# Modulation in units of 2048 columns, zero-padded half chunks, stick-breaking spread out, and two tiles computed together by chunk

## What is computed

```python
# first block, layer l (ctx is a second stream of 256 tokens, updated in layer 0 only)
mod = silu(c) @ w_mod[l] + b_mod[l]            # 1024 -> 6*1024, the same for ctx from c_ctx
sh1, sc1, g1, sh2, sc2, g2 = split(mod, 6)
h = rms_norm(x, norm1[l]) * (1 + sc1) + sh1
na_q, na_k, na_v, gq, gk, gv, ga, gb = split(h @ w_in[l])   # widths 512,512,512,512,128,128,1024,1024
ya = neighbourhood_and_ctx_attention(na_q, na_k, na_v)      # 8 heads
yb = softmax_attention(rope(norm(gq)), rope(norm(gk)), gv)  # 8 query, 2 key/value heads, x and ctx keys
x = x + g1 * ((sigmoid(ga) * (ya @ w_pa) + sigmoid(gb) * (yb @ w_pb)) @ w_o)
h2 = rms_norm(x, norm2[l]) * (1 + sc2) + sh2
x = x + g2 * ((silu(h2 @ w_a) * (h2 @ w_u)) @ w_out)        # hidden width 2816
# second block, layer l: half FFN, mixer, half FFN
x = x + 0.5 * ffn1(rmsnorm(x))
y_a = forgetting_attention(...)      # 6 heads
y_b = stick_breaking(...)            # 5 heads: log-sigmoids of the scores, summed over later keys
y_c = dsa(...)                       # 5 heads, keys of the top 64 by an index score
x = x + (g_a * (y_a @ w_up_fox) + g_b * (y_b @ w_up_sb) + g_c * (y_c @ w_up_dsa)) @ w_out
x = x + 0.5 * ffn2(rmsnorm(x))
```

## Time and profile before

| | |
|---|---|
| median of three runs | 2757.98 us |
| the profiled execution | 2758.39 us |
| its span in the trace | 2756.4 us |
| mean granted TensorE clock | 0.958 |
| TensorE busy | 2602.2 us (94%) |
| VectorE busy | 1367.5 us (50%) |
| ScalarE busy | 1144.9 us (42%) |
| GpSimd busy | 303.6 us (11%) |
| chain that ended last | TensorE 83%, ScalarE 7%, VectorE 6%, DMA 1% |

### The profile page before, as it was taken

One profiled execution on the slowest core, in us unless ns is written; L12 is line 12 of the kernel. 1 busy time (PEld: TensorE's weight loads), 2 busy tenths in 40 slices (PEclk: granted clock), 3 DMA queues, 4 the chain that ended last, 5 costly groups with the idle time before them and its releaser, 6 DMA issues.

```text
span 2756.4 us, 41454 instructions
## 1 busy us (share of the span) xinstructions
PE 2602.2 (94%) x17370; PEld 2281.8 (83%) x17370; DVE 1367.5 (50%) x2351; ACT 1144.9 (42%) x1970; POOL 303.6 (11%) x292
## 2 busy tenths in 40 slices
PE   4997999899999899989999998999999999999998
PEld 2763677677777687779999997889999998887998
DVE  2234434333333424555566556646556656665654
ACT  3242444322122424554454444445445444444543
POOL 1132411200000002410010000111000000022000
PEclk6997999899999889989999999989999999999999
DMA  5412222244443222235465452325545554333544
GB/s 223 177 54 94 75 77 92 92 183 164 180 183 132 90 85 90 80 123 183 167 207 184 168 193 99 131 100 170 184 168 198 179 173 155 115 118 137 182 166 140
DMA packets 60184, 393.44 MB, mean 143 GB/s; under 512 B 6688, under 2 KB 6848, under 8 KB 23520
## 3 DMA queue, kind: packets, MB, share of 16 engines
q1 hardware_dynamic: 59328, 384.45, 39.8%
q0 software_dynamic: 672, 6.36, 0.6%
HBM read 389.73 MB, written 1.05 MB: 142 GB/s over the span
## 4 chain that ended last, share of the span: by engine, by line
PE 83%; ACT 7%; DVE 6%; issue 2%; POOL 2%; DMA 1%; SPq 0%; DVEq 0%; POOLq 0%; ACTq 0%
PE ps L822 69%; PE ps L900 4%; DVE ring_lo L1459 3%; PE ps L972 2%; PE ps L863 2%; PE ps L957 2%; PE ps L946 1%; ACT w_hi L1109 1%; ACT logits L1249 1%; ACT prob_t L1164 1%; PE ps L873 1%; DMA ring<-w_mod 1%; PE ps L922 1%; DMA ring<-w_w_in 1%; PE ps L913 0%
## 5 line engine op out<-in xcount | busy, mean ns | idle before, releaser
L1459 DVE TENSOR_TENSOR ring_lo<-ring,w_hi 128x1024 fp32r<-128x1024 f32 (+3 forms) x712 | 764.6, 1115 | 553.1 <-ACT w_hi L1109 552.9
L822 PE MATMUL ps<-h_hi,w_hi 128*128 128x256 f32 (+1 forms) x3408 | 963.3, 314 | 30.5 <-ACT h_hi L1154 26.3
L822 PE MATMUL ps<-h_lo,w_hi 128*128 128x256 f32 (+1 forms) x3408 | 934.8, 307 | 0.0
L1109 ACT ACTIVATE w_hi<-ring 128x1024 fp32r<-128x1024 f32 (+3 forms) x712 | 642.7, 950 | 580.4 <-PE ps L822 232.8
L822 PEld LDWEIGHTS ps<-h_hi,w_hi 128*128 128x128 f32 x3408 | 654.5, 193 | 90.1 <-issue 31.0
L822 PEld LDWEIGHTS ps<-h_lo,w_hi 128*128 128x128 f32 x3408 | 652.7, 193 | 27.9
L822 PE MATMUL ps<-h_hi,ring_lo 128*128 128x256 f32 (+1 forms) x3408 | 558.3, 307 | 0.0
L822 PEld LDWEIGHTS ps<-h_hi,ring_lo 128*128 128x128 f32 x3408 | 484.8, 192 | 28.6
L822 PE MATMUL ps<-hid_hi,w_hi 128*128 128x256 f32 (+1 forms) x1056 | 284.2, 302 | 0.0
L822 PE MATMUL ps<-hid_lo,w_hi 128*128 128x256 f32 (+1 forms) x1056 | 283.4, 301 | 0.0
L1393 POOL TENSOR_SCALAR logits<-logits,stat 128x512 f32<-128x512 f32 (+2 forms) x140 | 161.3, 1165 | 738.2 <-DVE stat L1689 738.2
(11 more groups left out here) (222 smaller groups left out, 2435.8 us busy)
## 6 DMA issues: line engine op xcount, KB each, us to landing
ring<-w_ffn_in SPq DMA_DIRECT2D x132, 1024.0 KB, 4.8
ring<-w_ffn_out SPq DMA_DIRECT2D x96, 704.0 KB, 4.0
ring<-w_mod SPq DMA_DIRECT2D x48, 1024.0 KB, 6.8
ring<-w_in SPq DMA_DIRECT2D x42, 1024.0 KB, 4.8
ring<-w_w_in SPq DMA_DIRECT2D x30, 1024.0 KB, 4.9
ring<-w_up SPq DMA_DIRECT2D x16, 576.0 KB, 3.6
ring<-w_pab SPq DMA_DIRECT2D x8, 1024.0 KB, 4.8
ring<-w_wo SPq DMA_DIRECT2D x8, 1024.0 KB, 4.7
```

The source lines that it names most:

```text
L822: mm = pe.matmul(ps[f.bank][:, 0:n], (hi_w if wpart == "hi" else lo_w)[0:rows, at:at + P], hi if part == "hi" else lo, start=left == first ...
L1109: act.activation(w_hi[q.s % 2][:, h * n:(h + 1) * n], ring[q.slot][:, h * n:(h + 1) * n], ACT.Copy)\
L1459: dve.tensor_tensor(ring_lo[q.slot][:, c], ring[q.slot][:, c], plain(w_hi[q.s % 2][:, c]), ALU.subtract)\
```

## The change

- **Modulation.** A unit is 2048 columns of eight chunks; each chunk is one piece of four matmuls (one per group of 512 columns, each group in its own 32 array columns), all in bank 3, with one turn at the end (bank 4, N = 8, `row_sel` has 8 columns). There are 6 units instead of 24, 48 pieces as before. A piece's transfer takes four runs of 2 KB per partition instead of one of 8 KB. `some(unit, n)` puts n chunks at a place. Unit (0,0) stands at the start around the norm's row, (0,1) is spread two chunks behind each of the four neighbourhood products, (0,2) two behind each `merge1` item, three of layer 1 behind the last projection of layer 0's merge, 15 behind the gate/up products of layer 0's FFN, the last six behind layer 1's first norm and its first products. None stands in an attention.
- **Start.** The first norm is in two parts, the row and the scaling (`norm_row`) and `apply`; the statistics stand ahead of the modulation.
- **gv** is made feature by token like other tiles (24 matmuls, N = 512) into `spare` and turned by four transposes (`values`), ahead of `nav`.
- **Two tiles together.** The first product after a norm without a deferred norm, and the first of `w_o` or `w_out`, do two tiles at once, chunk by chunk; products with `need` are ordered chunk by chunk too.
- **Half chunks** 5 and 8 are filled with zeros (`y2_pad`) and their matmuls have 128 rows; vb has N = 330.
- **merged_rest** moves from VectorE to GpSimd.
- **Stick-breaking** is dealt out: `stick_ln` one tile later, the sums, products, fox biases and all index rounds between the va projection and the first four gate tiles. The attention begins at gate tile 4.

The core of the diff:

```diff
-        def mod_unit(l, u):
-            return add("mod", l=l, u=u, pieces=[piece(w["mod"][l][2 * u + k], SLOT, False) for k in range(2)],
-                       f=linear(), n=count("mod"))
-
-        def mod_turn(m):
-            add("mod_turn", l=m["l"], u=m["u"], of=m, f=fill(V_BANK))
+        feats, last_u, kv_last, units = {}, [None], [None], {}
+
+        def mod_unit(l, j):
+
+            f = fill(MOD_BANK)
+            for c in range(KC):
+                src = w["mod"][l].rearrange("(u k) p n -> k p u n", k=2)[c // 4][:, 4 * j:4 * j + 4, c % 4 * 512:(c % 4 + 1) * 512]
+                yield add("mod", l=l, j=j, c=c, p=piece(src, SLOT, False), f=f)
+            add("mod_turn", l=l, j=j, of=f, f=fill(TURN_BANK))
+
+        def some(unit, n):
+            for _ in range(n):
+                next(unit, None)
...
-                for u in range(4):
-                    mod_turn(mod_unit(0, u))
                 add("stats0", nxt=[prep(c, SQ, "stats") for c in range(KC)])
-            amps(l, 0)
-            full_norm(SQ, l, 0)
+                unit = mod_unit(0, 0)
+                some(unit, 5)
+                n = full_norm(SQ, 0, 0, ahead=True)
+                some(unit, 4)
+                amps(0, 0)
+                n["amp"] = plan.counts["amp"]
+                apply_norm(n)
+            else:
+                amps(l, 0)
+                full_norm(SQ, l, 0)
+                some(units[1, 2], 3)
...
+            def values():
+
+                run_all(feat("gvf", w["w_gv"][l][0], [0], SQ, length=KC * P))
+                feats["gv", 0] = fill(T_BANKS[1])
+                add("gv", f=feats["gv", 0], after=feats["gvf", 0])
...
+                unit = mod_unit(0, 1)
+                for t in nq + nk:
+                    run_all(t)
+                    if t is nq[0]:
+                        add("tables", n=1, after=feats["naq", 0])
+                        add("na_bias", l=0, n=0, after=feats["naq", 0])
+                    some(unit, 2)
+                values()
+                some(unit, 1)
...
+            mods = itertools.chain(units[1, 0], units[1, 1], itertools.islice(units[1, 2], 2))
...
-            add("stick_ln", n=5 * l, zs=zs)
+            add("index_round")
             t = chunks(2)
             next(t)
-            stick_acc(0, 1)
+            add("stick_ln", n=5 * l, zs=zs)
+            run_all(t)
+            add("index_round")
             fox(0)
-            run_all(t)
-            stick_acc(2, 3, 4)
-            fox(1)
+            stick_acc(1)
             tok(f"va{l}", w["va2"][l], 2, 4 * 384, 384, S, va2, scaled=True)
-            sv = [fill(V_BANK) for _ in range(3)]
-            for i, fv in enumerate(sv):
-                add("stick_pv", i=i, f=fv, n=5 * l)
-            fox(2, 3)
+            for _ in range(4):
+                add("index_round")
+            add("index_end", n=count("sel"))
+            stick_acc(0, 3)
...
                     if c == 0:
+                        stick_acc(2)
+                        fox(1)
+                    elif c == 1:
+                        stick_acc(4)
+                        stick_pv(0)
+                        fox(2)
+                    elif c == 2:
+                        stick_pv(1)
+                        fox(3)
+                    elif c == 3:
+                        stick_pv(2)
                         fox(4, 5)
-                    if 1 <= c <= 6:
-                        add("index_round")
-                    if c == 7:
-                        add("index_end", n=count("sel"))
-                    if c and c % 3:
+                    elif c % 3:
+                        if c < 6:
+                            stick_split(c - 4)
                         att(g)
+                    elif c == 6:
+                        stick_split(2)
...
-                pe.wait_ge(silu_c_ready, 1)
-                for k, p in enumerate(st["pieces"]):
-                    pe.wait_ge(landed[p.slot], p.landed)
-                    for g in range(4):
-                        mm = pe.matmul(ps[f.bank][32 * g:32 * g + 32, :], silu_c[:, (4 * k + g) * 32:(4 * k + g + 1) * 32],
-                                       ring[p.slot][:, g * 512:(g + 1) * 512], start=k == 0, stop=k == 1, skip_group_check=True)
-                        run(p, mm)
-                mm.then_inc(psum_full[f.bank], 1)
+                f, p, c = st["f"], st["p"], st["c"]
+                if c == 0:
+                    room(f)
+                    pe.wait_ge(silu_c_ready, 1)
+                pe.wait_ge(landed[p.slot], p.landed)
+                for g in range(4):
+                    mm = pe.matmul(ps[f.bank][32 * g:32 * g + 32, :], silu_c[:, c * 32:(c + 1) * 32],
+                                   ring[p.slot][:, g * 512:(g + 1) * 512], start=c == 0, stop=c == KC - 1, skip_group_check=True)
+                    run(p, mm)
+                if c == KC - 1:
...
+            def dve_norm_row(st):
+                dve_recip(st)
+                full(st["f2"])
+                for c in range(KC):
+                    scaled(st, c)
+
+            def dve_apply(st):
+                for c in range(KC):
+                    dve.wait_ge(h_hi_ready, st["base"] + c + 1)
+                    dve.tensor_tensor(at_T(h_lo, c, st["T"]), normed(st, c), plain(at_T(h_hi, c, st["T"])), ALU.subtract)\
+                        .then_inc(h_lo_ready, 1)
...
+                first = left[0]
                 for p, terms in groups:
                     hi_w, lo_w = w_hi[p.s % 2], ring_lo[p.slot]
-                    if fresh is not None:
-                        order = [("hi", "hi", t) for t in terms] + [("lo", "hi", t) for t in terms] + [("hi", "lo", t) for t in terms]
+                    if fresh is not None or need:
+                        order = [(*parts, t, k) for t in terms for parts in (("hi", "hi"), ("lo", "hi"), ("hi", "lo")) for k in range(len(fs))]
                     else:
-                        order = [("hi", part, t) for t in terms for part in ("hi", "lo")] + [("lo", "hi", t) for t in terms]
...
-                        rows = DH if c in (5, 8) else P
-                        terms.append((c * P, y2_hi[0:rows, c * S:(c + 1) * S], y2_lo[0:rows, c * S:(c + 1) * S], rows, c))
-                    product(f, S, [(st["p"], terms)])
+                        terms.append(([c * P], y2_hi[:, c * S:(c + 1) * S], y2_lo[:, c * S:(c + 1) * S], P, c))
+                    product([f], S, [(st["p"], terms)])
...
+            def dve_y2_pad(st):
+
+                full(st["after"])
+                for c in (5, 8):
+                    ins = dve.memset(y2[DH:P, c * S:(c + 1) * S], 0.0)
+                ins.then_inc(pad_ready, 1)
...
+                if m:
+                    merged_rest(st["mg"] - 1, m - 1)
+                if m == KC - 1:
+                    merged_rest(st["mg"], m)
+
+            def merged_rest(n, m):
+                pool.wait_ge(mg_hi_ready, n)
+                o = slice(m % 2 * S, (m % 2 + 1) * S)
+                pool.tensor_tensor(at_T(mg2_lo, m, S), tmp[0][:, o], plain(at_T(mg2_hi, m, S)), ALU.subtract).then_inc(mg_ready, 1)
```

272 lines of the change are left out of this document (143 added, 129 removed).

## The result

The changed kernel takes 2733.86 us (median of four runs, 2729.61 to 2735.67) against 2757.65 us before: ratio 0.9909, 95% interval 0.9893 to 0.9925. It is 24 us faster, where 73 were forecast, and lies outside the range of 2662 to 2720.

What follows compares the result with a forecast made beforehand. TensorE, busy 2602.2 of 2756.4 us, was taken as the bound, so less work or fewer idle and slow stretches would help. Terms summed to -73.7 us against 2758.39, giving 2685 us, range 2662 to 2720.

Steps and rivals of the forecast that it cites:

- the cover of modulation by the weight ring: Modulation chunks between weights: counted at 1.13 us of matmuls each, with late weight transfers counted in layer 0's merge.
- Merge and w_o: Layer 0's first merge: two chunks between steps and a later weight transfer make a step 16.3 us; +12.5 us.
- "+4": Layer 0's neighbourhood products: four pairs of chunks replace two units, +4 us, offset by -4 for gv.
- Second merge: Second block's merge: padded rows save matmul spacing, but the 5.82 us loop through other engines stays; -2.5 us.
- Attention: Layer 0's attention: four modulation units leave, with the transfer gap and idle time they cause; -15 us, bounds -8 and -21.
- gv of layer 1: Layer 1's gv: 18.77 us becomes 6.9, and some 3 us behind it if the clock stays up; -15 us.
- stick-breaking: Stick-breaking in both layers: waits and the low-clock stretch go, 3 us of new waits per layer; -16 us, 8 each.
- the start: Start of the kernel: squares no longer wait for the first weight copy, two tiles done at 66 us; -12 us.
- FFN and second norm of layer 0: Layer 0: chunks replace 14 units in the FFN, -22.5 us; chunks fill the second norm's idle time, -5 us.
- The root's delay: Layer 0's second norm: the weight copy now stands ahead of the root, costing up to 4 us.
- the waits only move: Rival: only removed TensorE work counts, attention -8, stick-breaking 0, first merge +17; -37 us, 2721 us; chance 0.23.
- Slow 2 KB rows: Rival: short rows make a modulation piece take 9.5 us; +57 us, 2815 us; chance 0.04, of which 0.03 slower.

Runs made afterwards that it cites:

- e1: Changed kernel with the split of the next weight pulled ahead only within two pieces, not three; 2728.17 us.
- e5: Changed kernel with the eight modulation chunks of layer 0's merge moved behind its four w_o items, two each; 2717.22 us.
- e9: Changed kernel with modulation chunks never two together from layer 0's merge on, and none ahead of its second norm or in layer 1; 2699.99 us.
- e2: Changed kernel with the tables and attention bias sent once the first norm's row is spread, not behind the first neighbourhood product; 2730.73 us.
- e10: e9 with the first weight split within the norm's apply, and tables and bias sent when gv is turned; 2683.72 us.
- e11: Changed kernel with stick-breaking, index rounds and forgetting biases in the order of the kernel before; 2736.45 us.
- e12: e10 with the mixer's last two attention steps moved from behind the last gate tile to gate tiles 6 and 9; 2677.34 us.
- e4: Changed kernel with the second merge's half chunks at 64 rows again, zeros still written; 2738.06 us.
- e7: Kernel before without its four modulation units in layer 0's attention, so part of the computation is left out; 2745.46 us.
- e8: Kernel before with gv made feature by token in both layers, in the places where it stood; 2745.53 us.

## Why the prediction was wrong

- **The failing step is the cover of modulation by the weight ring.** The forecast counted a chunk's matmuls (1.13 us; measured 1.00 and 0.17 in the FFN) and, in the merge, the late transfer. It did not ask at each place how far ahead the next weight is sent and split when two or three pieces of modulation stand in between. In the merge it took 6.8 us for the landing of the next weight; behind two chunks it is 9.6, and the split stands ahead of the evictions, so a step takes 20.4 us and not 16.3. Merge and w_o came out 15.2 us over the forecast: 12.2 from the three steps, and most of the rest behind the fourth item, where the sum had left out two chunks (1.85 us). e1 shows the order's part (2.5 us a step), e5 and e9 that the steps return to 12.3 and 13.7 us once no two chunks stand there. Among the neighbourhood products two chunks an item were called "+4" by their matmuls; the wait for a weight of 15.28 us, lengthened by tables and bias, made it +10 instead of 0 (e2, e10).
- **Second merge, -2.5 forecast, +3.1 measured.** Its sum left out the two attention steps that the new order puts between the last gate tile and the merge: with them in the gates it takes 8.9 us less (e11, e12). The padding itself is worth more than forecast, 4.2 us (e4), in the layer whose clock is low.
- **Attention, -15 forecast, -7.4 measured:** the near bound of 8, but not for its reason. Taking the units out frees 5.7 us of idle time; the clock, lower without them, takes back 9 of the 11.8 us of work (e7).
- **gv of layer 1, -15 forecast, about -10:** the gain in gv itself is right (18.77 to 7.2), the clock behind it was not freed (e8).
- **Right:** stick-breaking (-14.0 for -16, of which e11 shows 11.8 to be the order's), the start (-11.7 for -12), FFN and second norm of layer 0 (-25.7 for -27.5), vb (-1.9 for -2.2). The root's delay "up to 4" was 6.3.
- **The rivals:** "the waits only move" (2721) was nearer, 13 us below the measured time. It named the attention, gv and the merge, which are failing terms, but took nothing for stick-breaking, which gave 14.0. Slow 2 KB rows are excluded: 18432 more packets take (0.412 x 2731.2 - 0.398 x 2756.4) x 16 = 452 us of engine time more, 25 ns each, where that rival needed 296.
- Not separated by a run: how the 10 us around the neighbourhood products divide between chunks and the clock. From 66 to 130 us TensorE is idle for 7.1 us at a granted clock of 0.89; before it is never idle from 78 to 195, at 1.00.

## What to carry to other kernels

Where a side stream of transfers shares a ring with the weights, count at each place how many of its pieces stand between two weights: with one, the next weight here landed in 5.8 us and a merge step took 13.7; with two it was sent when the present item began, landed in 9.6 us, and the step took 20.4. Look at what an engine's "prepare the next" stands ahead of in its own order; work that waits for a transfer must not stand ahead of evictions that free banks. And when an edit reorders a stretch, follow what it moves to the stretch behind: the new order of stick-breaking gained 12 us there and cost the second merge 9, and the run's time alone would have called it worth 2.6.
